# Transitions by token block, weight homes outside the ring, and the experts' scatter from an exact 0/1 table

## What is computed

```
for i in range(2):                                    # first block
    h = rms_norm(x, attn_norm[i]); q, k, v, gates = split(h @ w_in[i])
    x = x + (g0*(ya @ w_pa) + g1*(yb @ w_pb) + g2*(yc @ w_pc)) @ w_out[i]
    h = rms_norm(x, mlp_norm[i])
    u = causal_conv(h @ w_up[i]); x = x + (silu(gate_u) * val_u) @ w_down[i]
for i in range(2):                                    # second block
    mix = hybrid_mixer(x, ...)                        # rwkv, conformer, short conv, gates
    x = layernorm(alpha * x + mix)
    f = swiglu(x) if i == 0 else moe_swiglu(x)        # 8 experts, top 2
    x = layernorm(alpha * x + f)
```

## Time and profile before

| | us |
|---|---|
| median of 3 runs | 2882.07 (2877.96 to 2884.68) |
| the profiled execution, its own time | 2881.7 |
| its span in the profile | 2879.9 |
| PE busy in the span | 2672.2 |
| DVE busy | 1821.1 |
| ACT busy | 1261.5 |

### The profile page before, as it was taken

How to read it: one execution, slowest core, us unless ns; L and a number is a source line. 1 busy time by engine, 2 the same in 40 slices (tenths; PEclk the granted TensorE clock), 3 DMA queues, 4 the chain that set the end, 5 groups by cost and what they waited for, 6 DMA issues and landing times.

```text
span 2879.9 us, 39065 instructions
## 1 busy us (share of the span) xinstructions
PE 2672.2 (93%) x15410; PEld 2278.7 (79%) x15410; DVE 1821.1 (63%) x2206; ACT 1261.5 (44%) x1440; POOL 145.7 (5%) x117
## 2 busy tenths in 40 slices
PE   7998998998899999988997999878999999999997
PEld 7875997886798888866997888747888888888885
DVE  5643775853676336534554355328888888888887
ACT  4441544451444321103334211116766766766665
POOL 1100000200000011200000023000000000000000
PEclk9998998999999999999998999979999999999998
DMA  6324443323454321125553211146988989898895
GB/s 245 109 103 156 176 181 117 132 103 122 171 193 159 128 92 45 59 91 192 180 189 118 102 59 45 44 190 263 362 338 340 360 335 343 343 363 335 340 346 187
DMA packets 76995, 558.31 MB, mean 194 GB/s; under 512 B 8640, under 2 KB 8768, under 8 KB 9536
## 3 DMA queue, kind: packets, MB, share of 16 engines
q1 hardware_dynamic: 76000, 551.19, 51.4%
q0 software_dynamic: 864, 5.24, 0.5%
HBM read 555.36 MB, written 1.05 MB: 193 GB/s over the span
## 4 chain that ended last, share of the span: by engine, by line
PE 54%; issue 33%; DVE 8%; ACT 2%; DMA 2%; POOL 1%; DVEq 0%; SPq 0%; POOLq 0%; ACTq 0%
PE bank L572 23%; PE bank L594 6%; PE bank L551 6%; PE bank L561 4%; PE bank L616 4%; DMA ring<-in_stream 2%; DVE yT L1788 1%; PE bank L581 1%; PE bank L822 1%; PE bank L833 1%; DVE x_lo L1455 1%; PE bank L692 1%; PE bank L676 1%; PE bank L675 0%; PE bank L684 0%
## 5 line engine op out<-in xcount | busy, mean ns | idle before, releaser
L2072 DVE TENSOR_TENSOR w_lo<-ring,w_hi 128x2048 fp32r<-128x2048 f32 x216 | 486.0, 2288 | 48.2 <-ACT w_hi L1402 48.1
L1402 ACT ACTIVATE w_hi<-ring 128x2048 fp32r<-128x2048 f32 x216 | 404.0, 1917 | 18.6 <-PE bank L996 16.7
L1464 DVE TENSOR_TENSOR w_lo<-ring,w_hi 128x2048 fp32r<-128x2048 f32 x99 | 226.8, 2291 | 161.0 <-ACT w_hi L1093 158.7
L996 PE MATMUL bank<-w_hi,xe_hi 128*128 128x512 f32 x792 | 312.3, 394 | 11.3 <-DVE w_lo L2072 9.3
L996 PE MATMUL bank<-w_lo,xe_hi 128*128 128x512 f32 x792 | 309.7, 391 | 0.0
L996 PE MATMUL bank<-w_hi,xe_lo 128*128 128x512 f32 x792 | 309.3, 390 | 0.0
L572 PE MATMUL bank<-x_hi,w_hi 128*128 128x256 f32 x1056 | 300.6, 285 | 5.5 <-DVE x_lo L1455 5.5
L1093 ACT ACTIVATE w_hi<-ring 128x2048 fp32r<-128x2048 f32 x99 | 189.3, 1912 | 260.6 <-DMA ring<-in_stream 155.3
L572 PE MATMUL bank<-x_lo,w_hi 128*128 128x256 f32 x1056 | 300.2, 284 | 0.0
L572 PE MATMUL bank<-x_hi,w_lo 128*128 128x256 f32 x1056 | 300.2, 284 | 0.0
L551 PE MATMUL bank<-xT,ring 128*128 128x256 f32 x1088 | 248.7, 387 | 1.1 <-ACT Z L1329 1.1
(11 more groups left out here) (342 smaller groups left out, 5176.5 us busy)
## 6 DMA issues: line engine op xcount, KB each, us to landing
ring<-in_stream SPq DMA_DIRECT2D x439, 1024.0 KB, 4.9
yT<-in_stream SPq DMA_DIRECT2D x54, 1024.0 KB, 6.5
xT<-in_stream SPq DMA_DIRECT2D x27, 1024.0 KB, 7.0
norm_rows<-in_rows POOLq DMA_DIRECT2D x4, 1024.0 KB, 6.0
cst<-in_cst SPq DMA_DIRECT2D x1, 2145.0 KB, 19.9
par<-in_par SPq DMA_DIRECT2D x1, 1502.0 KB, 15.3
xres<-in_x SPq DMA_DIRECT2D x1, 1024.0 KB, 5.2
group_rows<-in_rows POOLq DMA_DIRECT2D x2, 512.0 KB, 8.0
```

The costliest lines, as they stand in the source:

```text
L996: r = mm(banks[4 + j % 2], a[:, k, :], moe_part(b, i)[:, q * 512:(q + 1) * 512], start=(k == 0 and a is xe_hi and b is w_hi), stop=(k == K ...
L1402: act_(moe_part(w_hi, at), moe_slot(at), ACT.Copy).then_inc(*A.done("moe_hi", at))
L1464: v.tensor_tensor(part(w_lo, n), slot(f0 + n), part(w_hi, n).bitcast(F32), ALU.subtract)\
L2072: v.tensor_tensor(moe_part(w_lo, at), moe_slot(at), moe_part(w_hi, at).bitcast(F32), ALU.subtract)\
```

## The change

- **Weight homes.** Units 0 and 1 of every projection are loaded into two homes outside the ring (in Z, at 13312), not into a ring slot. The slots are counted without them, so that in the first block the ring already holds units 2 and 3 and two of the four w_out units when the projection starts. SP waits for the last user of that part of Z: `sumsq` 6 in the first block, the last `o` of the recurrence in the mixers. In the mixers the units are put in the order conformer, short convolution, rwkv. `project` waits for each unit where it is first used, and `project_out` unit n for the merge of its own columns.
- **Transitions by token block.** The last unit of each product that leads to a transition does tb 0 first, and signals it. DVE, ACT, POOL and PE then work on tb 0 while tb 1 is still being computed. Layer norms take their sum from the adding instruction itself (`accum_out`), not from an ACT pass. Transposes use banks 0, 1, 6, 7 and go block by block. The first product waits for each `x_lo` k by itself. x is loaded and the result stored in two halves.
- **Experts.** The column tables are worked out for all six tables in one instruction per q, while PE gathers. The weights multiply `y` before the scatter (`y_hi` by ACT, `y_lo` by DVE, both rounded), and `pickT` becomes an exact 0/1 table; the scatter is two rounded products in place of one float32 product. In the loop DVE makes `y_lo` at i == 4, behind two splits and a `hidden`.

The diff, cut to its core:

```
+def homes():
+
+
+    aside = {}
+    for l in range(DEPTH):
+        for n in range(2):
+            aside[l * LAYER1 + N_IN1 + n] = RING + n
+            aside[(MIX2_0, MIX2_1)[l] + N_IN2 + N_PROJ + n] = RING + n
+    out = []
+    for u in range(MOE_0):
+        out.append(aside.get(u, sum(v not in aside for v in range(u)) % RING))
+    return out
+
+
+HOME = homes()
...
-        s_x = ctx.enter_context(nc.semaphore("x_loaded"))
+        s_x = [ctx.enter_context(nc.semaphore(f"x{tb}_loaded")) for tb in range(TB)]
...
+        def home(h):
+            return ring[:, h * UNIT:(h + 1) * UNIT] if h < RING else Z[:, 13312 + (h - RING) * UNIT:13312 + (h - RING + 1) * UNIT]
+
         def slot(u):
-            return ring[:, (u % RING) * UNIT:(u % RING + 1) * UNIT]
+            return home(HOME[u])
 
         def slot_lo(u):
-            return ring_lo[:, (u % RING) * UNIT:(u % RING + 1) * UNIT]
+            return ring_lo[:, HOME[u] * UNIT:(HOME[u] + 1) * UNIT]
 
         def loaded(u):
-            return s_slot[u % RING], 16 * (u // RING + 1)
+            return s_slot[HOME[u]], 16 * HOME[:u + 1].count(HOME[u])
...
+        def turn_bank(k):
+            return banks[(0, 1, 6, 7)[k // 2]]
...
+        y_hi, y_lo = rounded("y_hi", 1024, D, gates_at), rounded("y_lo", 1024 + D, D, gates_at)
+        pick = gates[:, 3072:3328].rearrange("p (b n) -> p b n", b=TB)
+        pickw = gates[:, 3328:3584].rearrange("p (b n) -> p b n", b=TB)
+        pickT = rounded("pickT", 3584, TB * P, gates_at)
+        pickw_sum = gates[:, 3840:4096]
...
+                if HOME[u] in HOME[:u]:
+                    user = max(w for w in range(u) if HOME[w] == HOME[u])
+                    split = any(f <= user < f + FFN for f in ffn_starts)
+                    sp.wait_ge(*(V.of("lo", user) if split else T.of("unit", user)))
+                if HOME[u] >= RING:
+                    l = u // LAYER1 if u < MIX2_0 else int(u >= MIX2_1)
+                    sp.wait_ge(*(T.of("sumsq", l, len(QK_PAIRS) - 1) if u < MIX2_0 else T.of("o", l, 3)))
+                sp.dma_start(slot(u), stream[u]).then_inc(s_slot[HOME[u]], 16)
...
+            for tb in range(TB):
+                sp.wait_ge(*(V.of("x2", 1, tb) if n_stages == 4 else V.of("final")))
+                sp.dma_start(out_rows[:, tb, :], xr[:, tb, :]).then_inc(s_out, 16)
             if n_stages >= 3:
                 sp.wait_ge(*G.of("final"))
-            sp.dma_start(out_d.rearrange("(b p) n -> p b n", p=P), xr).then_inc(s_out, 16)
-            sp.wait_ge(s_out, 16)
+            sp.wait_ge(s_out, 32)
...
+                for tb in range(TB):
+                    pe.wait_ge(*ready[tb])
+                    for k in range(KT):
+                        at = (k % 2) * SEQ + tb * P
+                        t = nc.tensor.transpose(turn_bank(k)[:, at:at + P], src[:, tb, k * P:(k + 1) * P], ct("ident"))
+                        if tb:
+                            t.then_inc(*T.done("turned", tag, l, k))
...
+                order = [(c, tb) for tb in range(TB) for c in range(2)] if last else [(c, tb) for c in range(2) for tb in range(TB)]
+                for c, tb in order:
+                    for half in range(2):
+                        r = mm(banks[2 * tb + half], src(c)[:, tb * P:(tb + 1) * P],
+                               wv[:, c, half * 512:(half + 1) * 512], start=(first and c == 0),
+                               stop=(last and c == 1))
+                    if last and (c, tb) == (1, 0):
+                        r.then_inc(*T.done("rows", *key, 0))
...
+                        if ready and c == 0:
+                            pe.wait_ge(*ready(k))
...
+                unit_of = [(0, 1, 2, 3), (2, 3, 0, 1)][blk == "b2"]
+                here = set()
...
+                            u = u0 + unit_of[k // 2]
+                            if u not in here:
+                                pe.wait_ge(*loaded(u))
+                                here.add(u)
...
-                    pe.wait_ge(*V.of("merged", blk, l, 11))
+                    pe.wait_ge(*V.of("merged", blk, l, max(i for i, (c, b) in enumerate(BRANCHES[blk]) if c == n)))
                     at = 8 * BRANCHES[blk][0][1] + 2 * n
-                    rows(lambda c: gk[:, at + c, :], slot(u), n == 0, n == N_OUT - 1).then_inc(*T.done("unit", u))
+                    rows(lambda c: gk[:, at + c, :], slot(u), n == 0, n == N_OUT - 1, (blk, l)).then_inc(*T.done("unit", u))
...
+                    if n == 2:
+                        pe.wait_ge(*A.of("xT", "b2", l))
+                        pe.wait_ge(*V.of("xT", "b2", l))
...
+                        for y in (y_hi, y_lo):
+                            r = mm(out[half], pickT[:, tb * P:(tb + 1) * P], y[:, half * 512:(half + 1) * 512],
+                                   start=(y is y_hi), stop=(y is y_lo))
...
+                def y_high(half, key):
+                    act_(y_hi[:, half * 512:(half + 1) * 512], banks[half], ACT.Copy, scale=sm("slot_weight", 1)).then_inc(*key)
...
+                    for half in range(2):
+                        if peeled:
+                            act_(y_hi[:, half:half + 1], ct("ones", 0, 1), ACT.Copy).then_inc(*A.done("y", half))
+                        else:
+                            sc.wait_ge(*T.before("scattered", 1))
+                            sc.wait_ge(*T.before("moe_down", FJ - 1))
+                            y_high(half, A.done("y", half))
...
+                                sc.wait_ge(*V.of("y", 1))
+                                act_(pickw_sum, banks[7][:, 0:256], ACT.Copy, accum_out=sm("slot_weight", 1))\
+                                    .then_inc(*A.done("slot_weight"))
...
+            def rms_norm(tag, l, source):
+
+                if source:
+                    residual(*source, 0)
+                rms_mean(tag, l, 0)
+                if source:
+                    residual(*source, 1)
+                rms_apply(tag, l, 0)
+                rms_mean(tag, l, 1)
+                rms_apply(tag, l, 1)
...
+                def centre(tb):
+                    ve.wait_ge(*ready(tb))
+                    for half in range(2):
+                        add(tb, half, lnsum[:, 2 * tb + half:2 * tb + half + 1]).then_inc(*V.done("lnres", tag, l, tb))
+                    own()
+                    v.tensor_scalar(negmean[:, tb:tb + 1], lnsum[:, 2 * tb:2 * tb + 1], lnsum[:, 2 * tb + 1:2 * tb + 2],
+                                    -1.0 / D, ALU.add, ALU.mult).then_inc(*V.done("negmean", tag, l, tb))
...
+                centre(0)
+                variance(0)
+                centre(1)
+                scale(0)
+                variance(1)
+                scale(1)
...
+                for q in range(MORE):
+                    v.tensor_tensor(theirs[:, q, :, :], grow(mine[:, q, :], [P, 6, 8], 1), every[:, :, 0:8], ALU.mult)\
+                        .then_inc(*V.done("theirs"))
+                own()
+                v.tensor_reduce(sm("whom", MORE), which, AX.X, ALU.add).then_inc(*V.done("whom"))
+                for q in range(MORE):
+                    v.tensor_reduce(every[:, :, 8 + q:9 + q].rearrange("p t c -> p (t c)"), theirs[:, q, :, :], AX.X, ALU.add)\
+                        .then_inc(*V.done("column"))
+                own()
+                v.tensor_copy(turn_cells[:, 1:1 + MORE], sm("whom", MORE)[0:1, :]).then_inc(*V.done("cells"))
+                v.tensor_scalar(place[:, :, 8:8 + MORE], place[:, :, 8:8 + MORE], -float(P), None, ALU.add)\
+                    .then_inc(*V.done("cells"))
+                V.same(("turns",), ("cells",))
+                xe_low("xe0", "xe0")
...
+                def y_low(half, key):
+                    at = slice(half * 512, (half + 1) * 512)
+                    v.scalar_tensor_tensor(out=y_lo[:, at], in0=banks[half], scalar=sm("slot_weight", 1),
+                                           in1=y_hi[:, at].bitcast(F32), op0=ALU.mult, op1=ALU.subtract).then_inc(*key)
...
+                        if i == 4:
+                            for half in range(2):
+                                ve.wait_ge(*A.of("y", half))
+                                if peeled:
+                                    v.tensor_copy(y_lo[:, half:half + 1], ct("ones", 0, 1)).then_inc(*V.done("y", half))
+                                else:
+                                    y_low(half, V.done("y", half))
...
+                            if j == 9:
+                                ve.wait_ge(*A.of("slot_weight"))
+                                ve.wait_ge(*T.of("scattered", 1))
+                                v.tensor_scalar(pickT, banks[7][:, 0:256], 0.0, None, ALU.is_gt).then_inc(*V.done("pickT"))
...
-        for n in ("rwkv_w_o_2", "conf_w_o_2", "short_w_o_2", "w_out_2"):
+        for n in ("conf_w_o_2", "short_w_o_2", "rwkv_w_o_2", "w_out_2"):
```

346 lines of the change are left out of this document (141 added, 205 removed).

## The result

The changed kernel takes 2760.01 us (median of 4 runs, 2759.12 to 2767.62), the kernel before 2880.25 beside it (4 runs, 2877.96 to 2884.68): a ratio of 0.9587, 95% interval 0.9565 to 0.9608. That is 120 us less where 108 were forecast, inside the range of 2759 to 2798, but at its lower end. The profiled execution took 2759.35, its span 2757.5.

A forecast was written before the change was run, and what follows sets the result against it. PE was taken as the bound (busy 2672 of 2880 us), with its idle time, half clock and needless instructions to win. Savings 40.5 + 36.0 + 2.0 + 13.6 + 11.6 + 4.2 = 107.9 off 2881.7 gave 2774, range 2759 to 2798.

The forecast's parts named there:

- Waits for loads: Projections and w_out: PE's idle time falls by 28.7 us (5.6 + 19.4 + 3.7), by the weight homes.
- The clock: Half clock behind the load waits at projections and w_out: 11.8 us saved, called the least sure term.
- The rival in which the clock doesn't come back: Shorter gaps still put PE at half clock, so 11.8 + 2.3 shrink: 2788, chance 0.15.
- Transitions: Seven transitions by token block: 38.8 us saved, less 2.8 for hand-overs and clock, so 36.0.
- The replay: The transitions' old steps laid out by block: w_out to feed-forward saves 6.2 us, the router's layer norm 4.9.
- First turn: Experts' first turn, column tables under the gather: wait of 9.3, 2.0 of xe_lo, 2.3 of clock; 13.6 us.
- Scatter: Experts' loop, rounded scatter: 1.86 us less per turn, 0.4 lost to a wait, net 1.45; 11.6 in eight turns.
- End: From the last product to the span's end: rounded scatter and norm by block save 4.2 us.
- The loop that doesn't get faster: Experts' loop bound by loads or by a new wait at the turn's head: 11.6 us lost, 2785, chance 0.12.
- The slower case: Loop at i == 4: two y_lo delay the third split and loads; slower than before from 12 us a turn, chance 0.02.
- the likeliest case: Whole kernel: the forecast of 2774 us, own range 2767 to 2781, chance 0.48.
- The fifth rival: Replay and clock too cautious: no loop waits (3.2), no allowance (2.8), mixers' whole wait won (6.2): 2762, chance 0.10.

The follow-up runs named there:

- the changed kernel again: The changed kernel itself, nothing changed, run again on the chip of three later runs: 2765.39 us, ratio 0.9579 to the kernel before.
- The chain alone: The changed kernel with the column tables made serially again by about 70 small dependent instructions, behind xe_lo: 2776.49 us, ratio 0.9629 to the kernel before.

## Why the prediction was right, and where it was off

*Waits for loads.* The size was right, the reason was not: 29.3 of idle time where 28.7 were forecast. That it came out all the same is luck: the term counts the waits that go, whatever takes them away. The prediction put it down to the homes ("in the first block units 0 and 1 are loaded long before the projection"; in the mixers, loads "issued" after the last `o`). It took the mixers' homes for the projection's units, which they are not, and it overlooked that the change also releases each unit at its own last part. The runs show that waits and release by unit, with the mixers' new order, do it without the homes (kernel before with them: 0.4 of 34.8 left), and that leaving the homes out costs 0.3. The bound that did hold is ACT's gated yT: 3.09 of wait in the mixers, 1.85 less than 4.93, as worked out.

*The clock.* 11.8 forecast, 15.5 measured (in the first block 4.9 and 3.4, in the mixers 3.7 and 3.5 where 2 each stood). The mixers' term was too small. In most profiles it comes out as here, but the execution profiled as the changed kernel again ran 3.0 longer in one mixer, so a part of this term hangs on the execution. The rival in which the clock doesn't come back is refuted by 1.00 in both stretches of the first block.

*Transitions.* The replay gave 6.2 where 6.5 came, twice, 7.0 for 6.9 and 3.4 for 3.5: within 0.3. The layer norms gave 7.1, 6.2 and 5.6 for 6.2, 4.9 and 4.9. So of the 7.6 that are missing in this term, 2.9 are the replay of the layer norms, 0.5 that of the others, 1.4 lie behind the first product, and 2.8 are the allowance, taken off for hand-overs, reads of the sum and half clock. For the reads nothing was lost that shows: DVE's read of an accumulated sum takes 0.08, as in the first mixer's transition of the changed kernel:

```profile
1249.63 0.08 DVE L1769 DVE_READ_ACCUMULATOR xres<-xres,bank 128x1 f32 x1
```

Two parts were run alone: waiting for each `x_lo` by itself is worth 2.3 to 3.0 per place, block 0 first in the last unit 1.1 to 1.4. What working by block, `accum_out`, the order of the transposes and the halves of x are worth each is open.

*First turn.* 14.8 for 13.6. The chain alone is worth 13.6 by its experiment; the estimate of 9.3 and 2.3 fell short by its half clock.

*Scatter.* 1.45 a turn forecast, 1.12 measured. The gross gain was mis-sized: 0.46 per float32 instruction, from the duration of the group, which contains the last end. By starts it is 0.43, so 1.62 and not 1.86 (measured by itself: 1.62). The stall at the head was put at 0.4, and is 0.5 net of what the kernel before had there (moving `y_high` brought 0.72). ACT's `y_high` made it, not DVE's two `y_low`, which the prediction had named as well.

*End.* 7.2 for 4.2. From the last gather to the scatter it takes 12.4 where it took 12.1 (PE waits 2.9 for it); the scatter is 1.9 shorter, and from its last row to the end of the span 11.1 us pass where 16.7 did. The norm by block was under-priced.

*Rivals.* The loop that doesn't get faster fell, and with it the estimate of 101.5 us per turn: a turn of 33 transfers takes 99.12 at 347 GB/s, and 98.39 to 98.41 with `y_high` later. The Trainium skill, "DMA: Bandwidth & Descriptors", section "Measured (HBM→SBUF, 128 partitions, SWDGE, issued from GpSimd)", has the 341 GB/s behind that estimate for a transfer of 1 MB issued from GpSimd; here SP issues them, and the trace decides. The slower case never came near: DVE is busy for 87.9 of 99.1. Its counter-argument of three transfers under way at any time was too high: in the loop before, the 33 transfers of a turn landed a median of 5.9 to 7.2 us after issue, so about two were under way (an estimate).

*The range.* Transitions, clock and end were put too low, together 14.3 (7.6, 3.7, 3.0), the scatter 2.7 too high; the likeliest case was 14 us above the time. The fifth rival, "too cautious", gave 2762; its reasons (no stall in the loop, the mixers' whole wait won) were not the ones that came true, except for the missing allowance.

## What to carry to other kernels

Before buying memory for a prefetch, release and wait unit by unit, and put last in the order what is read last: here that brought 42 to 53 us of 2886, and the extra slots 0.3. Price pipelined instructions by the distance between starts, not by the duration of a group. An engine that is only 70% busy can still hold the one that bounds: a 1.3 us pair of copies at the head of ACT's turn cost 0.72 of a 99 us period, and moving it was free.

## What the runs showed of the hardware

The half clock after a wait isn't a constant of the program. The same 32 products behind the same 3.1 us wait took 7.17 in one execution and 10.21 in another (granted clock 1.00 and 0.69 over ten microseconds), and the profiled executions of the unchanged code up to the first projection took 180.1 to 184.7. That scatter is as large as the effects of single edits, so they can be told only by stretches at full clock. For one kernel the spans are 2757.5 and 2766.4 at mean clocks of 0.981 and 0.977. The Trainium skill, "TensorE: Matmul & The Clock Gate", section "What's actually happening", calls the number of slow products at the start of a kernel run-variable; these traces show it behind a wait in the middle of a kernel too.

A change of ACT's tables cost 1.28 each time, with the next instruction 0.01 to 0.02 behind its end (1187.86 + 1.28 and 1189.16), and two of them disappear in idle time.
